# Two buffers for the raw output weights in phase one, and the norm rows folded two steps later in phase two

## What is computed

```python
mod = silu(c) @ ada_w[l] + ada_b[l]
sh1, sc1, g1, sh2, sc2, g2 = split(mod, 6)
h = x * (1.0 + sc1) + sh1
z = h @ w_in[l] + b_in[l]
ya = _spatial_gating(gelu(z[..., :i1]), ...)         # chunks of 128 tokens, 4 heads
yb = _banded_gqa(q, k, v, sink, rel_bias)            # window of +-128 tokens
yc = _conformer_conv(z[..., i4:], ...)               # depthwise, 31 taps, then a norm and silu
y = concatenate([ya, yb, yc]) @ w_out[l] + b_out[l]
x = _layer_norm(ALPHA * x + (1.0 + g1) * y, ln_mix_g[l], ln_mix_b[l])
h = x * (1.0 + sc2) + sh2
y = _moe(h, ...)                                     # 32 experts, two of them per token
x = _layer_norm(ALPHA * x + (1.0 + g2) * y, ln_ffn_g[l], ln_ffn_b[l])
```

## Time and profile before

| | us |
|---|---|
| median of three runs (lowest, highest) | 2067.79 (2067.09, 2068.73) |
| the profiled execution's own time | 2067.05 |
| its span, from first to last instruction | 2065.3 |
| PE busy | 1672.9 (81%) |
| VectorE busy | 1340.5 (65%) |
| ScalarE busy | 988.0 (48%) |
| GpSimd busy | 275.4 (13%) |
| granted TensorE clock, mean, in parts of 2.4 GHz | 0.902 |

### The profile page before, as it was taken

The page is one execution under the profiler, slowest core; times in us unless marked ns, Lnnn a source line. Parts: engine busy times, 40 slices in busy tenths (PEclk is TensorE's granted clock), DMA queues, the critical chain, the costliest instruction groups (busy, mean ns, idle before and its releaser), DMA issues. The chain is left out here.

```text
span 2065.3 us, 28117 instructions
## 1 busy us (share of the span) xinstructions
PE 1672.9 (81%) x8080; PEld 1321.8 (64%) x8081; DVE 1340.5 (65%) x1992; ACT 988.0 (48%) x1542; POOL 275.4 (13%) x291
## 2 busy tenths in 40 slices
PE   3998669991699999993699999999999999995000
PEld 2776447861466777773578888888888888884000
DVE  5577657972356777775648786656557556473887
ACT  2212351222467777741647676645556456472221
POOL 0000000000000111112111101100000101100765
PEclk9999879995699999995799999999999999997555
DMA  7657453227233333212877977785768657459664
GB/s 298 220 194 260 127 203 113 82 72 286 105 110 110 108 103 103 93 66 80 334 296 284 420 292 300 291 345 227 283 231 348 261 212 279 180 212 310 219 223 152
DMA packets 136275, 435.36 MB, mean 211 GB/s; under 512 B 12577, under 2 KB 64033, under 8 KB 107540
## 3 DMA queue, kind: packets, MB, share of 16 engines
q1 hardware_dynamic: 111204, 349.69, 45.6%
q0 software_dynamic: 16944, 57.96, 8.2%
q10 hardware_dynamic: 8064, 26.92, 3.4%
HBM read 349.27 MB, written 87.34 MB: 211 GB/s over the span
## 5 line engine op out<-in xcount | busy, mean ns | idle before, releaser
L1969 DVE TENSOR_TENSOR gate_up_lo<-gate_up_raw,gate_up_hi 128x1024 fp32r<-128x1024 f32 x256 | 293.9, 1220 | 14.6 <-ACT gate_up_hi L1845 14.5
L1845 ACT CAST gate_up_hi<-gate_up_raw 128x1024 fp32r (+1 forms) x256 | 248.6, 1052 | 37.5 <-DMA gate_up_raw<-in_w_gate_up 33.4
L467 PE MATMUL proj_bank<-x_hi,w_hi 128*128 128x512 f32 x448 | 185.8, 415 | 40.6 <-DVE w_lo L579 34.2
L468 PE MATMUL proj_bank<-x_lo,w_hi 128*128 128x512 f32 x448 | 180.3, 402 | 0.0
L469 PE MATMUL proj_bank<-x_hi,w_lo 128*128 128x512 f32 x448 | 179.5, 401 | 0.0
L1781 PE MATMUL psum_gate<-gate_up_hi,x_hi 128*128 128x512 f32 x392 | 158.4, 404 | 12.8 <-DVE x_lo L1969 8.6
L1795 PE MATMUL psum_y<-down_hi,h_hi 128*128 128x512 f32 x392 | 158.9, 405 | 7.0 <-DVE h_lo L1969 7.0
L1969 DVE TENSOR_TENSOR down_lo<-down_raw,down_hi 128x1024 fp32r<-128x1024 f32 x128 | 150.6, 1222 | 9.4 <-ACT down_hi L1853 5.9
L645 DVE SCALAR_TENSOR_TENSOR conv<-y_win,cw,conv 128x1008 f32<-128x1008 f32 (+1 forms) x120 | 154.1, 1284 | 3.0
L1782 PE MATMUL psum_gate<-gate_up_lo,x_hi 128*128 128x512 f32 x392 | 154.2, 393 | 0.0
L1783 PE MATMUL psum_up<-gate_up_hi,x_hi 128*128 128x512 f32 x392 | 154.2, 393 | 0.0
(11 more groups left out here) (279 smaller groups left out, 3491.5 us busy)
## 6 DMA issues: line engine op xcount, KB each, us to landing
gate_up_raw<-in_w_gate_up SPq DMA_DIRECT2D x128, 1024.0 KB, 11.4
down_raw<-in_w_down SPq DMA_DIRECT2D x64, 1024.0 KB, 6.9
expert_outputs<-y_rows ACTq DMA_DIRECT2D x49, 512.0 KB, 6.8
x_raw<-in_ada_w SPq DMA_DIRECT2D x16, 1024.0 KB, 4.8
w_raw<-in_w_in SPq DMA_DIRECT2D x28, 512.0 KB, 5.6
x_raw<-in_xT SPq DMA_DIRECT2D x16, 512.0 KB, 9.2
q_kept<-q_stage SPq DMA_DIRECT2D x32, 256.0 KB, 2.8
q_tile<-q_kept SPq DMA_DIRECT2D x16, 512.0 KB, 3.9
```

The lines of the kernel that those rows point to most:

```text
L467: mm(bank[:, :], w_hi[side][:, k, :], x_hi[m][:, k, :], start=(k == 0), stop=False)
L468: mm(bank[:, :], w_hi[side][:, k, :], x_lo[m][:, k, :], start=False, stop=False)
L1845: nc.scalar.copy(gu_hi[:, k, :], raw_chunk(slot, k)).then_inc(gu_high_ready, 1)
L1969: return tt(out, raw, high.bitcast(F32), ALU.subtract)
```

## The change

In phase one the raw row k is loaded into `gelu_v` or into `v_nat` by turns. The rows 0 and 1 are loaded ahead of the loop; in turn k GpSimd loads row k+1 before it waits for row k's split, and the load waits only for the low part of row k-1, which lies in the same buffer. Landed loads and stored low parts have a semaphore for each buffer, stored high parts one of their own, and the high cast waits only for the stored high part of the row before. The scaling, the cast and the split stand at the same units as before. Block 2 of the spatial gating waits in `finish_sgu` until the low parts in `v_nat` are stored. In phase two the three folding instructions, with the wait for the four rows, move from step 0 (ahead of `invert_sums`) to step 2 (behind `shift_mean`).

```diff
-        wo_stage = gelu_v[:, :, :].rearrange("p a b -> p (a b)")
+        wo_stage = [x[:, :, :].rearrange("p a b -> p (a b)") for x in (gelu_v, v_nat)]
...
                 dve.wait_ge(v_rstd_ready, macro + 1)
+                if macro == 2:
+                    dve.wait_ge(wo_lo_stored[1], 16 * (WO_ROWS // 2))
...
                             dve.wait_ge(wo_high, k + 1)
-                            low(wo_stage.bitcast(F32R), wo_stage, wo_stage_hi).then_inc(wo_low, 1)
+                            stage = wo_stage[k % 2]
+                            low(stage.bitcast(F32R), stage, wo_stage_hi).then_inc(wo_low, 1)
...
-                            dve.wait_ge(wo_landed, 16 * (k + 1))
-                            tt(wo_stage, wo_stage, gain1, ALU.mult).then_inc(wo_scaled, 1)
+                            dve.wait_ge(wo_landed[k % 2], 16 * (k // 2 + 1))
+                            tt(wo_stage[k % 2], wo_stage[k % 2], gain1, ALU.mult).then_inc(wo_scaled, 1)
...
                     if macro == 2:
-                        act.wait_ge(wo_stored, 32 * WO_ROWS)
+                        act.wait_ge(wo_hi_stored, 16 * WO_ROWS)
+                        act.wait_ge(wo_lo_stored[0], 16 * (WO_ROWS - WO_ROWS // 2))
...
                     if k > 0:
-                        act.wait_ge(wo_stored, 32 * k)
-                    nc.scalar.copy(wo_stage_hi.bitcast(F32R), wo_stage).then_inc(wo_high, 1)
+                        act.wait_ge(wo_hi_stored, 16 * k)
+                    nc.scalar.copy(wo_stage_hi.bitcast(F32R), wo_stage[k % 2]).then_inc(wo_high, 1)
...
+                    pool.wait_ge(mix_filled, 2)
+
+                    def load_wo(k):
+                        if k >= 2:
+                            pool.wait_ge(wo_lo_stored[k % 2], 16 * (k // 2))
+                        pool.dma_start(wo_stage[k % 2], io["w_out"][:, k, :] if k < DC else io["b_out"]
+                                       ).then_inc(wo_landed[k % 2], 16)
+
+                    load_wo(0)
                     for k in range(WO_ROWS):
-                        if k > 0:
-                            pool.wait_ge(wo_stored, 32 * k)
-                        pool.dma_start(wo_stage, io["w_out"][:, k, :] if k < DC else io["b_out"]
-                                       ).then_inc(wo_landed, 16)
+                        if k + 1 < WO_ROWS:
+                            load_wo(k + 1)
                         pool.wait_ge(wo_low, k + 1)
-                        pool.dma_start(io["wo"][k, :, 0, :], wo_stage_hi).then_inc(wo_stored, 16)
-                        pool.dma_start(io["wo"][k, :, 1, :], wo_stage).then_inc(wo_stored, 16)
+                        pool.dma_start(io["wo"][k, :, 0, :], wo_stage_hi).then_inc(wo_hi_stored, 16)
+                        pool.dma_start(io["wo"][k, :, 1, :], wo_stage[k % 2]).then_inc(wo_lo_stored[k % 2], 16)
...
-                if s == 0:
-                    dve.wait_ge(rows_landed, 64)
-                    tt(h2[:, :], x1_shift[:, :], h2_gain[:, :], ALU.mult).then_inc(setup_steps, 1)
...
                 if out is not None:
                     shift_mean(out)
+                if s == 2:
+                    dve.wait_ge(rows_landed, 64)
+                    tt(h2[:, :], x1_shift[:, :], h2_gain[:, :], ALU.mult).then_inc(setup_steps, 1)
```

More of the change, by code:

```diff
@@ L275, in project_tokens @@
             sem("toe_filled"), sem("toe_ready"), sem("toe_stored"), sem("toe_spread"))
-        gain_landed, wo_landed, wo_scaled, wo_high, wo_low, wo_stored = (
-            sem("gain_landed"), sem("wo_landed"), sem("wo_scaled"), sem("wo_high"), sem("wo_low"), sem("wo_stored"))
+        gain_landed, wo_scaled, wo_high, wo_low, wo_hi_stored = (
+            sem("gain_landed"), sem("wo_scaled"), sem("wo_high"), sem("wo_low"), sem("wo_hi_stored"))
+        wo_landed = [sem(f"wo_raw_landed_{i}") for i in range(2)]
+        wo_lo_stored = [sem(f"wo_lo_stored_{i}") for i in range(2)]
         bias_filled, bias_ready = sem("bias_filled"), sem("bias_ready")
@@ L973, in _ @@
                     pool.dma_start(gain1, io["mods"][0:1, :].to_broadcast([P, D])).then_inc(gain_landed, 16)
+                    pool.wait_ge(mix_filled, 2)
[5 more added lines that the diff above has]
+                    load_wo(0)
                     for k in range(WO_ROWS):
-                        if k > 0:
-                            pool.wait_ge(wo_stored, 32 * k)
-                        pool.dma_start(wo_stage, io["w_out"][:, k, :] if k < DC else io["b_out"]
-                                       ).then_inc(wo_landed, 16)
+                        if k + 1 < WO_ROWS:
+                            load_wo(k + 1)
                         pool.wait_ge(wo_low, k + 1)
-                        pool.dma_start(io["wo"][k, :, 0, :], wo_stage_hi).then_inc(wo_stored, 16)
-                        pool.dma_start(io["wo"][k, :, 1, :], wo_stage).then_inc(wo_stored, 16)
-            pool.wait_ge(wo_stored, 32 * WO_ROWS)
+                        pool.dma_start(io["wo"][k, :, 0, :], wo_stage_hi).then_inc(wo_hi_stored, 16)
+                        pool.dma_start(io["wo"][k, :, 1, :], wo_stage[k % 2]).then_inc(wo_lo_stored[k % 2], 16)
+            pool.wait_ge(wo_hi_stored, 16 * WO_ROWS)
+            for i in range(2):
+                pool.wait_ge(wo_lo_stored[i], 16 * ((WO_ROWS + 1 - i) // 2))
 def attend_tokens(nc, io, keep):
@@ L1500, in _ @@
                         advance(parts, 4)
-                if s == 0:
-                    dve.wait_ge(rows_landed, 64)
-                    tt(h2[:, :], x1_shift[:, :], h2_gain[:, :], ALU.mult).then_inc(setup_steps, 1)
-                    dve.wait_ge(setup_steps, 3)
-                    tt(h2_shift[:, :], h2_shift[:, :], h2[:, :], ALU.add).then_inc(setup_steps, 1)
-                    tt(h2_gain[:, :], h2_gain[:, :], x1_gain[:, :], ALU.mult).then_inc(setup_steps, 1)
-                    dve.wait_ge(setup_steps, 5)
                 if z is not None:
@@ L1516, in _ @@
                     shift_mean(out)
+                if s == 2:
+                    dve.wait_ge(rows_landed, 64)
+                    tt(h2[:, :], x1_shift[:, :], h2_gain[:, :], ALU.mult).then_inc(setup_steps, 1)
+                    dve.wait_ge(setup_steps, 3)
+                    tt(h2_shift[:, :], h2_shift[:, :], h2[:, :], ALU.add).then_inc(setup_steps, 1)
+                    tt(h2_gain[:, :], h2_gain[:, :], x1_gain[:, :], ALU.mult).then_inc(setup_steps, 1)
+                    dve.wait_ge(setup_steps, 5)
                 advance(parts, 2 if pair_at(s, 5) is not None else 40)
```

## The result

The changed kernel takes **2014.99 us** (median of 4 runs, 2012.87 to 2018.69) where the kernel before takes 2067.44 beside it (2066.16 to 2068.73): a ratio of 0.9748, 95% interval 0.9731 to 0.9765. The profile that is read here is that of the slowest of the four: 2018.69 us by its own time, span 2017.0, against 2067.05 and 2065.3 before. The span fell by 48.3 us. The medians differ by 52.4 us, so this trace, 3.7 us above its median, shows less of the gain than the median does.

The account below looks back on a forecast made before the run. VectorE's waits for loads were taken to bound it: 41.2 us for raw rows in phase one, 21.94 for four rows in phase two. 34.0 + 21.2 = 55.2 off 2067.05 gave 2011.9, about 2012 us; range 2003 to 2023.

Parts of the forecast that it names:

- Phase one, norm of the first half: Units 17 to 24: VectorE's three waits for raw-row loads (6.03, 5.47, 5.73 us) go, 17.2 us gained.
- Only 7.6 us, the maximum, would show, by some 1 us: Phase one, high cast waiting for the stored high part: median landing of 3.3 us hidden, only the slowest would show.
- Units 25 to 28: Phase one, up to ScalarE's first scaling of the fourth block: 28.3 us gained in all so far, 26.7 to 29.9.
- Units 29 to 36: Phase one, VectorE's waits at rows 7 and 8, first kept only in part: 5.8 us gained, 5.3 to 6.4.
- Phase one in all: Sum of phase one's terms, 28.3 + 5.8: 34 us gained, bounds 29 and 41.
- Phase two: Step 0 ends 24.3 us earlier, 3.1 return as PE's wait for the third `q_tile`: 21.2 us, 17.6 to 24.3.
- The fold at no cost: Phase two, before step 3's first scores: folding overruns by 1.5 us, covered by PE's output projection matmuls; taken as 0.
- A: Phase one: ScalarE's high cast waits for the high part's store in most rounds; some 24 kept, 2022 us; chance 0.12.
- B: GpSimd's transfers land only when VectorE pauses; only phase two pays, 2046.6 us; chance 0.03, shared with another rival.
- D: Both phases pay whole, 41.2 + 24.3 = 65.5 us: 2002 us; chance 0.05.
- E: Slower than before: lower granted TensorE clock in the experts, about 2079 us at 0.91; chance 0.02.
- C: Phase two held by transfers: third `q_tile` lands 3.6 us later still, 2016 us; counted within the forecast's 0.78.

Follow-up runs that it names:

- the fold alone: Only phase two's fold moved to the end of step 2, one raw buffer as before, on the kernel before: 2047.88 us, ratio 0.9916.
- the fold inside step 2: Changed kernel with the three fold instructions behind the second pair of scores of step 2 instead of at its end: 2014.29 us, ratio 0.9754.

## Why the prediction came out as it did

The forecast was 2012.0, the measurement 2014.99, and the signs and places were right. The terms are held against the trace of the slowest run, which gained 48.3 us of the 55.2 forecast; the median gained 52.4. So of the 6.9 us that the terms below miss, some four belong to this one run. The error has one main term, the likeliest value of the stretch up to the fourth block.

**Phase one, norm of the first half: 17.2 forecast.** The three waits went as told. The trace of after has 15.7, the five other traces with the same phase one 16.3 to 16.9 by the same cut. About 1.0 us of the 1.5 missing came with the first load, for which the prediction had no term: issued with a second one behind it, it landed after 8.4 us where it took 7.4 before. "Only 7.6 us, the maximum, would show, by some 1 us" was right for the price and wrong for how often: row 1's high part, for which the cast of row 2 waits, issued at 193.73 beside `q_stage`'s stores from SyncE, took 6.6 us, ScalarE stood 7.23, and VectorE 0.74 behind it. It wasn't a slow landing by chance: in the seven traces with this order of stores it took 6.2 to 6.7, where the kernel before has 3.3.

**Units 25 to 28: 28.3, bounds 26.7 to 29.9.** This is the step that failed. The first scaling of the fourth block came 24.0 us earlier (25.8 and 25.9 in the two traces beside the fold alone). The 7.6 us that I called the slow end of the store of row 4's high part was what this transfer takes in this company. It is issued 0.44 us behind the input block in both kernels; it took 7.6 and 7.8 us with one buffer, and 7.5 to 8.8 in the seven traces with two, 8.7 in the one that is read here, from 244.97 on. No transfer of 2.9 us was to be had there, so the sum should have stood at its lower bound, 26.7. And 28.3 is no value "nearer the slow end": it is the middle of 26.7 and 29.9. What is missing below 26.7 is the 1.5 us of the first term and 1.1 us for 8.7 in place of 7.6.

One row was misread. The earlier trace rows holds the landings of the third block of tokens, issued at 162.68; those of the fourth, issued at 259.70, were:

```profile
DMA to landing us min/median/max: 5.7/9.1/10.4
```

So its first piece would have been there at 248.2 and not at 250.5, and the store alone held ScalarE. The sum came out the same, since both had been put at 250.5; but only by the right row can the fast end be reached. It was real: with the high part's store out of the input block's way the first scaling came 29.4 us earlier than in the trace of before and 28.5 earlier than in that of the fold alone, on the same chip, and the store landed in 2.9 us, as the fastest of the earlier trace rows.

**Units 29 to 36: 5.8.** From the fourth block to the end of phase one the trace gained 5.3. On the other chip the same cut gives 2.5 and 2.7, because the kernel with one buffer was itself 3 us faster there in this stretch (204.15 against 207.29), with the same instructions. This term isn't told more closely than that.

**Phase one in all: 34, bounds 29 to 41.** 28.8 us by the start of phase two, 29.3 counted from the first load, at the lower bound, which was put there for just this ("two more us given back to slow landings twice"). The likeliest value should have been nearer to it. The wait forecast for ScalarE at row 5, 2 to 5 us, was 6.05 here and 4.9 to 6.2 in the other traces of this order; the one at row 2 was not forecast.

**Phase two: 24.3 - 3.1 = 21.2.** Step 0: 24.3. The wait for `q_tile`: 3.9 us, the tile 19.7 us on its way where 19.3 stood in the earlier trace rows. At the end of the attention 21.3 were left. The fit is partly luck: 1.4 us came back at the start of step 3, where the granted clock stayed at its upper level, of which the prediction says nothing, and 0.5 us went again in the steps behind. The fold at no cost was right, and the fold inside step 2 bears it out.

**Not forecast:** the bands at the start of phase two landed 0.4 us later, and 1.3 us went behind the sums of step 15. Both lie within the scatter of the traces (9.5 to 11.4 us for the bands, 1168.9 to 1173.4 for the stretch behind).

**The rivals.** A had the right mechanism at about half its size: it put 10 us on it (24 kept of 34), the order of the stores was worth 4.6, and ScalarE waited in two of eight rounds, not in most. B is out: behind the first load no transfer from GpSimd held VectorE, and the stores that were slow were those beside others. Its sign, loads or stores of over 8 us, did show (8.7 and 10.7 us beside the input block), but it was a poor sign: the low part at the same place took 9.7 us in the kernel before. By the Trainium skill, SBUF — State Buffer, "SBUF: two separate sides", they should be slow where VectorE runs in a mode that holds the port it shares with GpSimd; the prediction stretched that to any VectorE without pauses. Here, with the store sent early, the high part of row 4 landed in 2.9 us while VectorE was busy with subtractions from 234.04 to 238.95 without a pause, and in 8.7 beside the input block. Whether those subtractions run in such a mode no trace shows, so the rule is neither borne out nor refuted. D (both pay whole, 2002) is out by the waits that stayed. E is out at a clock of 0.99 in the experts on both sides. In C the inputs of the next tile were queued early, at 488.70, as feared, but behind the third `q_tile`, which took 0.4 us longer and not 3.6.

## What to carry to other kernels

When a single staging buffer gets a second one, look at once for the buffer behind it that stays single, and give each consumer the store that it needs and no other: a part that is ready should leave when it is ready, not with its pair. Price a transfer by one that travels beside the same others, and don't average it with faster ones that travelled alone: the one slow store of nine was slow because of where it stood, and there it was slow again. Check that a row of landings belongs to the transfer that it is used for. Where the edit recovered a wait of TensorE, one trace showed 1.5 us of its 3.9 two steps on, and three traces the whole of it on the mean thirteen steps later; judge such a gain on several traces.

## What was not expected of the hardware

- A store of 512 KB from GpSimd took 2.9 us with little beside it and 8.7 us beside 2 MB of input and 1 MB of weights (7.5 to 8.8 over seven traces). The Trainium skill, DMA: Bandwidth & Descriptors, "Anatomy of one DMA — SWDGE (gpsimd) path", gives some two us and the bytes at 436 GB/s for one such transfer; the 3.2 us that follow from it, an estimate, agree with the fast case only.
- A transfer placed earlier in a full queue doesn't travel faster (19.4 and 19.7 us); it landed earlier by about the time of what it was put ahead of, 4.9 us for 2 MB.
- The first piece of the input block landed after 5.6 or 5.7 us in every one of the thirteen traces, whatever stores travelled beside it; the high part's store was what became slow.
- TensorE's granted clock was 0.50 or 1.00 in the third and fourth us behind one and the same pause of 1.70 us at the start of step 3. It was 0.50 in five of the six traces whose step 2 had no stop, and 1.00 in the six with a stop of 3.4 to 4.4 us; a stop of 3.15 us went with 0.50, and one trace without a stop had 1.00.
- Runs of one kernel spread by up to 11.4 us over a group of runs (2058.8 to 2070.3 for the kernel before), where the first three lay within 1.7.
